# Admitting the recurrence's work items five in every twelve turns instead of one in every two

## What is computed

```python
def step(state, xs):                      # per chunk, 8 heads of 64
    qc, kc, gc, vc = xs
    cum = jnp.cumsum(gc, axis=2)
    ...
    scores = jnp.einsum('bhtk,bhsk,bhtsk->bhts', qc, kc, decay)
    o = (jnp.einsum('bhts,bhsv->bhtv', scores, vc)
         + jnp.einsum('bhtk,bhkv->bhtv', qc * jnp.exp(cum), state))
    ...
o = o * lax.rsqrt(jnp.mean(o * o, axis=-1, keepdims=True) + EPS)
merged = (jax.nn.sigmoid(gate_sb) * (y_sb @ w_branch_sb)
          + jax.nn.sigmoid(gate_hg) * (y_hg @ w_branch_hg))
```

## Time and profile before

| | us |
|---|---|
| median of 3 runs | 1609.47 |
| lowest and highest run | 1607.25, 1610.89 |
| span of the profiled execution | 1605.4 |
| PE busy | 1557.0 (97%) |
| DVE busy | 1022.6 (64%) |
| ACT busy | 818.1 (51%) |
| POOL busy | 209.4 (13%) |

### The profile page before, as it was taken

How to read it: one execution, slowest core, us unless ns; L and a number is a source line. 1 busy time by engine, 2 the same in 40 slices (tenths; PEclk the granted TensorE clock), 3 DMA queues, 4 the chain that set the end, 5 groups by cost and what they waited for, 6 DMA issues and landing times.

```text
span 1605.4 us, 20111 instructions
## 1 busy us (share of the span) xinstructions
PE 1557.0 (97%) x7908; PEld 1252.7 (78%) x7908; DVE 1022.6 (64%) x1689; ACT 818.1 (51%) x1425; POOL 209.4 (13%) x282
## 2 busy tenths in 40 slices
PE   9999999989999999999999999999999999999999
PEld 7877677678787888888777766878767988888887
DVE  4267966775648999989887786565765334333331
ACT  5278775435455888888864434323334333333220
POOL 1000014530343200000063111111101000000000
PEclk9999999999999999999999999999999999999999
DMA  6122121114626999999853111031122232323232
GB/s 245 54 78 79 53 79 53 38 43 147 236 83 242 319 421 423 421 421 420 311 215 105 53 53 53 27 105 53 54 78 79 79 105 81 103 92 100 84 106 92
DMA packets 78641, 236.19 MB, mean 147 GB/s; under 512 B 6960, under 2 KB 9296, under 8 KB 66256
## 3 DMA queue, kind: packets, MB, share of 16 engines
q1 hardware_dynamic: 68288, 207.91, 35.8%
q10 hardware_dynamic: 6624, 14.88, 2.5%
q0 software_dynamic: 3632, 12.08, 2.0%
HBM read 222.26 MB, written 12.60 MB: 146 GB/s over the span
## 4 chain that ended last, share of the span: by engine, by line
PE 81%; DVE 12%; ACT 4%; issue 1%; DMA 1%; POOL 1%; SPq 0%; DVEq 0%; ACTq 0%; POOLq 0%
PE bank L107 77%; PE bank L110 4%; DVE REST L122 2%; DVE low L132 2%; ACT REST L113 1%; DVE REST L132 1%; DVE REST L135 1%; ACT CHH L116 1%; DVE low L122 1%; DVE REST L144 1%; ACT REST L116 1%; DVE REST L141 1%; DVE REST L128 1%; DVE st L138 1%; POOL st L122 1%
## 5 line engine op out<-in xcount | busy, mean ns | idle before, releaser
L122 DVE TENSOR_TENSOR low<-slot,CHH 128x1024 fp32r<-128x1024 f32 (+1 forms) x300 | 296.1, 1029 | 114.2 <-ACT CHH L116 113.2
L116 ACT ACTIVATE CHH<-slot 128x1024 fp32r<-128x1024 f32 (+1 forms) x300 | 259.0, 901 | 130.3 <-PE bank L107 57.4
L132 DVE SCALAR_TENSOR_TENSOR low<-slot,smalls,CHH 128x512 fp32r<-128x512 f32 (+1 forms) x232 | 169.1, 759 | 190.4 <-ACT CHH L116 190.2
L107 PE MATMUL bank<-AH,CHH 128*128 128x512 f32 (+1 forms) x640 | 250.0, 391 | 0.2 <-DVE AL L122 0.2
L107 PE MATMUL bank<-AL,CHH 128*128 128x512 f32 (+1 forms) x640 | 243.1, 380 | 0.0
L107 PE MATMUL bank<-AH,low 128*128 128x512 f32 (+1 forms) x640 | 242.8, 379 | 0.0
L116 ACT ACTIVATE CHH<-slot,smalls 128x512 fp32r<-128x512 f32 (+1 forms) x232 | 154.7, 701 | 137.4 <-PE bank L107 68.4
L107 PE MATMUL bank<-CHH,AH 128*128 128x512 f32 x512 | 216.7, 423 | 3.1 <-ACT REST L116 2.0
L107 PE MATMUL bank<-low,AH 128*128 128x512 f32 x512 | 201.5, 394 | 0.0
L107 PE MATMUL bank<-CHH,AL 128*128 128x512 f32 x512 | 201.0, 393 | 0.0
L107 PE MATMUL bank<-CHH,XTF 128*128 128x512 f32 x512 | 161.3, 396 | 1.9 <-DVE REST L119 1.1
(11 more groups left out here) (177 smaller groups left out, 2352.8 us busy)
## 6 DMA issues: line engine op xcount, KB each, us to landing
slot<-in_w_in SPq DMA_DIRECT2D x35, 1024.0 KB, 5.2
slot<-in_w_exp_gate SPq DMA_DIRECT2D x32, 1024.0 KB, 12.1
slot<-in_w_exp_up SPq DMA_DIRECT2D x32, 1024.0 KB, 11.7
slot<-in_w_exp_down SPq DMA_DIRECT2D x32, 1024.0 KB, 12.0
slot<-in_w_gate SPq DMA_DIRECT2D x10, 1024.0 KB, 5.0
slot<-in_w_up SPq DMA_DIRECT2D x10, 1024.0 KB, 5.1
slot<-in_w_down SPq DMA_DIRECT2D x10, 1024.0 KB, 5.0
slot<-in_w_out SPq DMA_DIRECT2D x8, 1024.0 KB, 5.2
```

The lines of the kernel that those rows point to most:

```text
L107: return self.e.matmul(out, l, r, start=start, stop=stop) if self.e else Issued()
L116: return self.e.activation(out, in_, ACT.Copy, scale=scale) if self.e else Issued()
L122: return self.e.tensor_tensor(out, a, b, op) if self.e else Issued()
L132: return self.e.scalar_tensor_tensor(out=out, in0=a, scalar=s, in1=b, op0=op0, op1=op1) if self.e else Issued()
```

## The change

`HG_EVERY` becomes the triple `12, 0, 5`, which all four places pass on to `staggered` as `every`, `turn` and `of`. An item is admitted in turns of which `turn * of % every` is less than `of`: with 12 and 5 these are turns 3, 5, 8, 10 and 12 of each twelve, before it was every second turn. A pair's ten items are thus spread over 24 turns instead of 20.

```diff
-HG_EVERY = 2
+HG_EVERY = 12, 0, 5
...
-def staggered(items, width, every=1, turn=0):
+def staggered(items, width, every=1, turn=0, of=1):
     active, items = [], list(items)
     while items or active:
         turn += 1
-        if items and len(active) < width and turn % every == 0:
+        if items and len(active) < width and turn * of % every < of:
             active.append(items.pop(0))
...
-        hg_gen = staggered(hg_items(hg_begin, hg_level, hg_end), 5, HG_EVERY)
+        hg_gen = staggered(hg_items(hg_begin, hg_level, hg_end), 5, *HG_EVERY)
```

More of the change, by code:

```diff
@@ L3002, in hg_end @@
             yield from pause(HG_LAST[p] + 2)
-        drain(staggered(hg_items(hg_begin, hg_level, hg_end), 5, HG_EVERY))
+        drain(staggered(hg_items(hg_begin, hg_level, hg_end), 5, *HG_EVERY))
         for f in range(KT):
```

## The result

| | us |
|---|---|
| kernel before, median of 5 runs (lowest, highest) | 1608.0 (1607.04, 1610.89) |
| changed kernel, median of 5 runs (lowest, highest) | 1633.0 (1630.58, 1635.02) |
| ratio, with its 95% interval | 1.0148 (1.0137 to 1.0159) |
| span of the profiled execution, before and after | 1605.4 and 1630.7 |

A forecast was written before the change was run, and what follows sets the result against it. PE was taken as the bound, busy 1557.0 of 1605.4 us; waits of +13.2 us and one clock fall of +2.9 made +16.1 on 1609.5, rounded to 1625.5 us, range 1617 to 1634.

The forecast's parts named there:

- Term 1: Last pair's levels 4 to 7, in turns without dense steps: waits of 7.5 us instead of 1.6, 13.2 us in all.
- Terms 2 and 3: After each read-out, y_hg transposition waits 2.0 us, three times, +3.9; level 0 of pairs 1 to 3 waits 0.6, +1.8.
- Term 4: Level 3 of each pair waits for ACT's eight copies of level 2, 1.9 us in the last pair: together +2.4.
- Term 5: Waits won in pair 0 and at levels 4 to 6 of pairs 0 to 2; level 7 keeps 0.6: -2.4 us.
- Term 6: Tail of the last pair: Kd transposition +0.5 us, y_hg transposition waits 1.5 instead of 0.4, +1.1.
- The sum at full clock: Added waits of Term 1 to Term 6 together, with the clock at 2.4 GHz: +13.2 us.
- Term 7: One fall of PE's clock to 1.2 GHz in the empty turns: +2.9 us, from a span of 1.8 to about 4.
- Rival C: Clock falls again and again, in the empty turns and on 2 us waits: +24 us, 1633 us; chance 0.13.
- B: Same waits as forecast, but no fall of the clock: +13.2 us, 1622.7 us; chance 0.22.
- F: Waits milder, K never late and the chain after the read-out a microsecond shorter: +7 us, 1616.5 us; chance 0.06.
- D: More turns per pair relieve DVE, ACT and POOL, removing all steady waits: -3.6 us, 1605.9 us; chance 0.04.
- E: Lost time is given back in the DMA-held expert stage, where loads catch up: 1610 us; chance 0.05.

The follow-up runs named there:

- unread matmuls at every long wait: Changed kernel plus matmuls whose result nobody reads in nine empty turns and ahead of the other waits over 1.5 us: 1625.94 us (1.0096).
- the gap alone: Kernel before, still one item every second turn, but HG_AT 24 instead of 8, leaving ten turns without a dense step: 1624.97 us (1.0101).
- five in eleven: Changed kernel with HG_EVERY 11, 0, 5 instead of 12, 0, 5, leaving two empty turns: 1620.51 us (1.0067).
- the kernel before with the later transposition: Kernel before with HG_LAST 2 instead of 1 for pairs 0 to 2, y_hg transposition one turn later: 1611.45 us against 1610.24 (1.0013).
- `bs0` early: Changed kernel, but bs0 begins at turn 89 and fills the empty turns 89 to 98: 1630.11 us (1.0118).
- `before_again`: Kernel before, unchanged, run once more for a second profile: 1608.01 us.

## Why the prediction was right, and where it was not

**Term 1, the empty turns: right.** 7.5 us of waits were worked out for levels 4 to 7 and 7.03 measured (1.99 + 1.51 + 2.03 + 1.50), two for L122 and two for L144 as said. The 13.2 us from level 3 to `bs0` at full clock are 13.22 in the kernel with unread matmuls at every long wait, of which up to 0.4 is the filling, which overshoots two of the waits; from the changed kernel's own waits it would be 5.7 + 7.0 = 12.7 (an estimate). At half clock they are 17.25.

**Terms 2 and 3: right.** Three waits of 1.87 us at L110 (predicted 2.0); level 0 of pairs 1 to 3 waits 0.53, 0.52 and 0.55 (predicted 0.6).

**Term 4: right in its large part.** Level 3 of the last pair waits 1.78 (predicted 1.9). The others together have 0.8, as before, so the term was 1.8 and not 2.4.

**Term 5: one part missed.** Levels 4 to 6 of pairs 0 to 2 keep 1.1 us (predicted 1.6). But level 7 of pair 0 was to keep its 0.6 and waits 2.05. The timelines of ACT and DVE in the changed kernel:

```profile
261.46 1.97 ACT L116 ACTIVATE R<-bank 128x512 f32<-128x512 f32 x3 [0.88 <-PE bank L107]
...
263.95 0.71 ACT L116 ACTIVATE CHH<-slot,smalls 128x512 fp32r<-128x512 f32 x1
```
```profile
264.69 0.75 DVE L132 SCALAR_TENSOR_TENSOR low<-slot,smalls,CHH 128x512 fp32r<-128x512 f32 x1 [2.14 <-ACT CHH L116]
265.36 1.33 DVE L144 COPY_PREDICATED REST<-masks,bank 128x512 f32<-128x512 uint8 x2
```

The level now falls on the end of `gs1`, where ACT evacuates three banks before it splits the next chunk; DVE's low part of that chunk stands ahead of the copies and waits 2.14 us for ACT. I had compared DVE's order around pairs 1 to 3 and taken pair 0 for alike. With this the term is about -1.5, not -2.4.

**Term 6: half.** The last y_hg transposition waits 1.43 (predicted 1.5). The Kd transposition has no wait, since at half clock the three dense steps ahead of it took longer; at full clock it waits 0.31.

**The sum at full clock: right.** Waits 22.6 against the 24.3 of the prediction and 11.1 before; +12.8 us in the kernel that keeps the clock up, against +13.2. That so close a figure came out is partly chance: terms 1, 2, 4 and 6 were each a little too dear and term 5 promised 0.9 too much, so the waits themselves come to some 11.8 us at full clock (11.5, and the 0.31 of term 6), and 12.8 holds the overshoot of the filling.

**Term 7, the clock: the mis-sized term.** It had +2.9 for one fall. By the end of `bs1` it is 9.2 us by the run with unread matmuls, 22.0 - 11.5 = 10.5 by the growth of the waits alone. That run's filling overshoots two waits by 0.2 us each and so prices the clock too low; at half clock a wait of 0.31 is hidden (term 6), so that the growth of the waits prices it too high. The two figures lie on either side of it. By rows: four groups at 2.08 for 1.16 make 3.7, level 3 at 1.97 another 0.8, the first eight dense matmuls of `bs0` (3.5 us from 383.94 on, where a pitch of 0.23 would make 1.9) another 1.6, together 6.1 in the empty turns; three single stretches leave 4.4, or 1.5 each, a little under the 1.8 of the earlier trace rows. The step that failed is "one fall": I took the wait of 2.82 us without a sequel for a sign that such waits are mostly harmless, and counted one fall for the eight long waits of terms 1, 2 and 4. The change made ten waits of 1.43 to 2.05 us where none had been over 1.0; of the four that stand alone among dense steps before the empty turns (2.05 and three of 1.87) three had a stretch behind them. In the empty turns PE went on from wait to wait with 2.08 us of work between and the clock stayed down. Rival C had priced just this: 8 + 2.7 = 10.7 us. The page of the Trainium skill that the prediction cites (TensorE: Matmul & The Clock Gate, section HAM oscillation — how this bites in real kernels) has a kernel with short bursts of matmuls between waits that is throttled each time. The traces agree for the pattern, with 20.4 us at 0.50, but the waits in that page's example are some 3 to 5 us long, and those here only 1.5 to 2.05 us. The premise at the prediction's start, that a new order can only make PE's waits fewer or more, is where the size got lost: half of the loss is the same matmuls at half clock.

**The rivals.** B (no fall) and F (milder waits) are refuted by the windows and the list of waits. D (relief decides) would have needed a shorter chain after the read-out, which the three waits of 1.87 exclude. C has the time, 1633, but in part by luck: its +24 had nothing for the 3.3 us far behind the change, and the stretch that it priced came to +22.0. E (given back later) is refuted: the distance to the kernel before grows from 22.0 to 25.3 us. That growth was in no case of mine. It stands at 500, 848 and 1076 us in stretches at half clock, one of them:

```profile
1076.80:1080.20 3.40, 3.40 (x15) 3.11 (x15) 0.67 (x2) 1.30 (x3) 0.00 (x0) 0.50 0.00 0
```

It follows a wait that was there before but grew, from 1.35 to 2.19 us. This wait is 1.34 to 1.38 us in five executions (the two of the kernel before, the gap alone, five in eleven, and the kernel before with the later transposition), one of which has a stretch at half clock behind it; in the other seven it is 1.95 to 2.19 us, and all seven have one. Behind `bs1` the kernels lose between 0.7 (five in eleven) and 7.9 us (`bs0` early) more; the one with unread matmuls at every long wait loses 7.2. What makes these later waits longer stays open, and `before_again` shows that the same wait can go either way.

## What to carry to other kernels

Items that are interleaved with dense steps by counting turns need a count of both: 98 turns beside 88 steps leave the last ones in a row, and there each level costs its chain (2.7 to 3.35 us) and not PE's 1.15. When a change gives PE waits of about 2 us among dense steps, price each as its length and a chance of well over a half of another 1.5 to 1.8 us at half clock (of 24 single waits of 1.85 to 3.27 us in the recurrence, ahead of the empty turns, in eight traces, 17 had a stretch behind them), and several of them with little work between as one long stretch at half clock. Before giving a gap dense work from elsewhere, look what that work hides at its old place: here five DMA issues in a row, 9.8 us on ACT's queue.

## What the runs showed of the hardware that I had not expected

- The lower clock can last as long as the pattern does: 20.4 us at 0.50 with level groups of 2.08 us between waits of 1.5 to 2.0 us. Twenty-seven matmuls without a reader cut this to 3.4 us and the kernel by 3.3 us; fifty-seven, at the single waits too, left none in this part and cut the kernel by 7.1 us.
- Whether a wait is followed by the lower clock is not a property of the wait alone: 1.96 us without and 1.98 us with it at the same instruction of the same kernel, and 2.82 and 3.27 us without.
- One DMA issue of 2 KB held ACT's queue for 7.39 us while three larger ones ahead of it took 0.40 to 0.67. In the other traces the third takes 1.39 to 2.97 and the fourth 4.51 to 5.26; what holds them no run shows.
